# Constants, short loads and bands moved from the set-up into the first FFN, and half of the first weight tiles issued by ScalarE's queue

## The chip, the cores and the metric

The kernel runs on one NeuronCore of a Trainium2 chip, as one program. The metric is the device time in microseconds (us) of one execution; less is better. A core has TensorE (matrix products into PSUM, called PE in the profile, with PEld for its weight loads), VectorE (DVE), ScalarE (ACT), GpSimd (POOL) and SyncE (SP). SP, ACT and POOL also issue transfers, each to a queue of its own (q1, q10 and q0 in the profile), and 16 DMA engines serve all queues.

## The reference

Two transformer-like blocks follow each other on 256 tokens of width 1024, in float32. The first has two layers; beside the tokens `h` it carries 256 context tokens `hc`. Each layer takes nine modulation vectors per stream from `silu(c) @ w_ada`, and is an FFN, a mixer and a second FFN:

```python
# per layer of the first block, m and mc = silu(c) @ w_ada + b_ada for tokens and context
h = post(h, swiglu(pre(h, m, 0, 0), ffn_wi[0], ffn_wo[0]), m, 0, 1, 0.5)
...
h = post(h, o @ w_o, m, 3, 3, 1.0)
h = post(h, swiglu(pre(h, m, 6, 4), ffn_wi[1], ffn_wo[1]), m, 6, 5, 0.5)
```

`pre` is an RMS norm with scale and shift from `m`, `post` a gated residual. The mixer is attention with head gains `qk_g`, rotary tables and, for a group of heads, a relative position bias from `rpb` inside a window; the kernel reads that bias as "bands". The second block is an SSD and mLSTM mixer, a gated linear attention and convolutional FFNs; of it only the small parameters `ab_d_skip`, `ab_dt_bias`, `ab_ig_bias`, `ab_fg_bias` and `ab_a_log` matter here.

## The kernel before

Weights stream through a ring of two slots of 128 x 4096 floats (`RING`, `SLOT`). A float32 product is made of three products of rounded parts: ScalarE copies half a slot (a granule) to `wh` (L453), VectorE subtracts to get `wl` (L458), and TensorE multiplies `uh` x `wh`, `ul` x `wh`, `uh` x `wl` (L467 to L469). Every stage is a block with a program for each engine and a barrier at its end.

**The set-up** (`setup`, L512 on) is the first stage. It needs the token rows, some vectors, and the first six tiles of `w_ada` for layer 0 (1024 rows x 384 columns, 1536 KB each; tiles 0 and 1 in the ring's slots, 2 to 5 in the arena). SP's queue issues the identity (`const[:, 0:P]`, L534), the early vectors (L536), the six ada tiles (L538), and then the two first tiles of the first FFN's weights (L423), each as soon as TensorE is through with the ada tile that held its slot. ScalarE's queue issues four token loads of 512 KB (L618, L619). ScalarE then makes `silu(c)` in `act_c` (L622, L623), issues the rest of the constants (L626, all columns from 128 to 2175) and eight short loads: `head_gain` and `d_skip` twice each with elements of four bytes (L628, L631), three parts of `gate_bias` (L635) and `a_log` (L636). After that it squares the turned tokens (L642). Pool issues the late vectors (L547).

TensorE multiplies `act_c` with one ada tile after the other (`ada_rows`, L666, eight products of 32 output rows each, seen as 16 instructions), turns tokens between the tiles (L568), sums the squares with the constant `ones` after tile 3 (L573; it waits for `const_loaded`), turns the late vectors after tile 4 (L579) and at the end turns the ada rows into columns (L673). VectorE copies the turned tokens to `h` (L603), scales `head_gain` (L610) and puts the modulation vectors into `mod` (L679, L686). Then the barrier comes.

**The first FFN** is `ffn1(0, 0, ...)` (L1248), the next stage. Its norm scales `h` (L826), applies scale and shift on ScalarE (L777), and splits the input into `uh` (L801) and `ul` (L835); before that ScalarE needs the first weight tile (L453), on which VectorE's `wl` and then the first product wait. It has 22 granules of two groups of 128 output columns each; `prod` counts them. Between granules TensorE multiplies one further ada tile (L666). There is one slot for these tiles: ScalarE issues the next (L703) when the products of the last are done, and TensorE needs it after the next granule. Pool runs `load_bands` (L1599) from the stage's start: a flip matrix, a zeroed DRAM buffer (L1607), the `rpb` rows written into it (L1610), each waited for, and then 24 transfers of 64 KB (L1618) from the buffer to `bands`, in runs of 256 bytes. The mixer after this FFN reads them. `ffn1(1, 0, ...)` of layer 1 does the same without ada tiles.

Of the kernel before, what the change touches and what calls it, by code (L numbers as in the profile page):

```python
# [159 lines left out]
def two_blocks(nc, a, out, stop=None):  # L160
    ctx = ExitStack()
    with ctx:
# [4 lines left out]
        def sb(name, shape, dt=F32, at=None):  # L167
            size = 4 * int(np.prod(shape[1:]))
            offset = place[0] if at is None else at
            if at is None:  # L170
                place[0] += (size + 31) // 32 * 32
            return nc.alloc_sbuf_tensor_at(name, shape, dt, offset=offset)

        def signal(name):
            return Signal(ctx.enter_context(nc.semaphore(name)))
# [84 lines left out]
        def col(name, i, n=1):  # L260
# [31 lines left out]
        gelu_done = signal("gelu_done")  # L292
        ada_loaded, ada_multiplied, ada_copied, ada_turned, ada_summed, ada_taken = (signal(n) for n in (
            "ada_tile_loaded", "ada_tile_multiplied", "ada_rows_copied", "ada_columns_made", "ada_columns_summed", "ada_columns_taken"))
        first_loaded, late_loaded, tokens_loaded, const_loaded, gain_loaded, x_squared, x_added, x_summed = (signal(n) for n in (
            "first_vectors_loaded", "late_vectors_loaded", "tokens_loaded", "const_loaded", "gains_loaded", "x_squared", "x_squares_added", "x_summed"))
        low_turned, low_copied, low_weight_loaded, gates_made, gates_biased, gates_softened, decays_summed, decays_made, keys_ended, ends_turned = (
            signal(n) for n in ("low_rank_turned", "low_rank_copied", "low_rank_weight_loaded", "gates_made", "gates_biased", "gates_softened",
                                "decays_summed", "decays_made", "keys_ended", "ended_keys_turned"))
# [172 lines left out]
        def with_lead(eng, n, lead, body, first=0, most=None):  # L472

            turns(eng, n - lead, 4, lambda turn, k: body(turn, k, True), first, most)
            for g in range(n - lead, n):
                body(g // 4, g % 4, False)
# [33 lines left out]
        def setup():  # L512
# [18 lines left out]
            with stage() as block:  # L531
                @block.sync
                def _(sp):
                    sp.dma_start(const[:, 0:P], a["const"][:, 0:P]).then_inc(first_loaded.sem, 16)  # L534
                    for v, t, r, m in early:
                        sp.dma_start(rows[r:r + m, t, :], v).then_inc(first_loaded.sem, 16)  # L536
                    for i in range(ADA_FIRST):
                        sp.dma_start(tiles[i], w_ada[:, :, i * ADA_COLS:(i + 1) * ADA_COLS]).then_inc(ada_ready[i].sem, 16)  # L538
                    for i in range(RING):
                        sp.wait_ge(ada_multiplied.sem, ada_multiplied.at(i + 1))  # L540
                        load(sp, plan[first_key], i, i)
# [7 lines left out]
                @block.tensor  # L549
                def _(pe):  # L550
                    def turned(g):
                        if g >= 3:
                            pe.wait_ge(dve_free.sem, dve_free.at(g - 2))

                    pe.wait_ge(first_loaded.sem, first_loaded.at(16 * (1 + len(early))))
                    for t in range(EARLY):
                        pe.transpose(ps[:, bank_of(t), 0:P], rows[:, t, :], ident).then_inc(prod.sem, 1)
                    pe.wait_ge(act_free.sem, act_free.at(8))
                    for i in range(ADA_FIRST):
                        pe.wait_ge(ada_ready[i].sem, ada_ready[i].at(16))  # L560
                        ada_rows(pe, 0, tiles[i], i, i == 0, i == ADA_FIRST - 1).then_inc(ada_multiplied.sem, 1)
                        for j in TOKENS.get(i, ()):
                            g = EARLY + j
                            if j == 0:
                                pe.wait_ge(tokens_loaded.sem, tokens_loaded.at(16 * 2 * ST))
                            turned(g)
                            for t in range(2 * ST):
                                last = pe.transpose(ps[:, bank_of(g), t * P:(t + 1) * P], tokens[:, t, j * P:(j + 1) * P], ident)  # L568
                            last.then_inc(prod.sem, 1)
                        if i == SUM_AFTER:  # L570
                            pe.wait_ge(const_loaded.sem, const_loaded.at(16))
                            pe.wait_ge(x_added.sem, x_added.at(KD - 1))
                            pe.matmul(ps[:, 7, :], ones, sq_of(0), start=True, stop=True).then_inc(x_summed.sem, 1)  # L573
                        if i == LATE_AFTER:
                            pe.wait_ge(late_loaded.sem, late_loaded.at(16 * len(late)))
                            for t in range(EARLY, len(row_tiles)):
                                g, m = KD + t, row_tiles[t]
                                turned(g)
                                pe.transpose(ps[:, bank_of(g), 0:m], rows[0:m, t, :], ident[0:m, 0:m]).then_inc(prod.sem, 1)  # L579
                    pe.wait_ge(ada_copied.sem, ada_copied.at(1))  # L580
                    ada_columns(pe, 1, mod_rows).then_inc(ada_turned.sem, 1)

                @block.vector
                def _(dve):
# [21 lines left out]
                    add_square(KD - 1)  # L606
                    for t in range(EARLY, len(row_tiles)):
                        take_cols(KD + t, t)
                    dve.wait_ge(gain_loaded.sem, gain_loaded.at(16 * 8))
                    dve.tensor_scalar(head_gain[:, 0::2], head_gain[:, 0::2], HD ** -0.5, None, ALU.mult)  # L610
                    dve.wait_ge(ada_turned.sem, ada_turned.at(1))
                    dve_chain.link(dve, ada_sum(dve, 1, mod_sums))
                    ada_take(dve, mod_sums, 0, ADA_FIRST).then_inc(ada_taken.sem, 1)
# [2 lines left out]
                def _(act):  # L616
                    for t in range(ST):
                        act.dma_start(tokens[:, t, :], a["x"][0, t * P:(t + 1) * P, :]).then_inc(tokens_loaded.sem, 16)  # L618
                        act.dma_start(tokens[:, ST + t, :], a["ctx"][0, t * P:(t + 1) * P, :]).then_inc(tokens_loaded.sem, 16)  # L619
                    act.wait_ge(dve_free.sem, dve_free.at(1))  # L620
                    act.wait_ge(pool_step.sem, pool_step.at(1))
                    act.activation(act_c[:, :, 30], col("c", 0, KD), ACT.Silu).then_inc(act_free.sem, 1)  # L622
                    act.activation(act_c[:, :, 31], col("c_ctx", 0, KD), ACT.Silu).then_inc(act_free.sem, 1)  # L623
                    for _ in range(6):
                        act.nop().then_inc(act_free.sem, 1)
                    act.dma_start(const[:, P:CONST_W], a["const"][:, P:CONST_W]).then_inc(const_loaded.sem, 16)  # L626
                    for half in range(2):
                        act.dma_start(head_gain[half * HD:(half + 1) * HD, :],  # L628
                                      a["qk_g"].rearrange("l i d -> d (l i)"),
                                      allow_slow_non_contiguous=True).then_inc(gain_loaded.sem, 16)  # L630
                        act.dma_start(d_skip[half * HD:(half + 1) * HD, :],  # L631
                                      bass.AP(a["ab_d_skip_2"].tensor, half, [[0, HD], [2, KD]]),
                                      allow_slow_non_contiguous=True).then_inc(gain_loaded.sem, 16)
                    for v, at, n in ((a["ab_dt_bias_2"], 0, 32), (a["ab_ig_bias_2"], 32, 16), (a["ab_fg_bias_2"], 48, 16)):
                        act.dma_start(gate_bias[:, at:at + n], bass.AP(v.tensor, 0, [[0, P], [1, n]])).then_inc(gain_loaded.sem, 16)  # L635
                    act.dma_start(a_log[:, :], bass.AP(a["ab_a_log_2"].tensor, 0, [[0, P], [1, 32]])).then_inc(gain_loaded.sem, 16)  # L636
                    act.preload_act_table_set(LN_EXP)
                    for k in range(KD):
                        act.wait_ge(dve_free.sem, dve_free.at(EARLY + k + 1))
# [605 lines left out]

        spare_beside_bands, spare_of_bands = spare_input("spare_beside_bands", ADA.start), spare_input("spare_of_bands", MID.at)

        def ffn1(l, f, norm, tail, bands_of=None, ada=None, spare=None):  # L1248


            T = norm.T
            key = ("up", l, f)
            down = Down(key, ("down", l, f), mid, T, tail, dve_free, ada, spare)
            pairs = 4 if ada is None else 2
            with stage() as block:
# [40 lines left out]
                def _(dve):  # L1296
# [14 lines left out]
                            down.low_ahead(dve, 1)  # L1311
                    norm.vector(dve, lambda g: low_of(0, g))
                    with_lead(dve, KF, 2, granule)
                    if ada is not None:
                        ada.sums(dve)
                        ada.vector(dve)
                    down.vector(dve)

                @block.gpsimd
                def _(pool):  # L1320
                    if bands_of is not None:
                        load_bands(pool, bands_of)
            norm.done()
            if ada is not None:
                ada.done()
# [1 line left out]
            down.done()  # L1327
            dve_free.passed(KF)
            gate_done.passed(KF)
            if bands_of is not None:  # L1330
                pool_step.passed(1)
                flip_load.passed(16)
                band_load.passed(16 * (2 + B_HEADS * ROWS))
# [261 lines left out]
        assert CC_END <= MID.at and RB.at <= ARENA - (KD + 1) * ADA_COLS and AM.at <= ARENA - B_HEADS * ST * S  # L1595
        bias = Arena(ARENA - B_HEADS * ST * S).take(B_HEADS, ST, S)
        softs = sb("softs", [P, 24])

        def load_bands(pool, l):  # L1599

# [1792 lines left out]
```

## Time and profile before

| | before |
|---|---|
| median of 3 runs | 2850.27 us (2848.3 to 2850.82) |
| profiled execution | 2851.26 us, its span 2849.4 us |
| mean granted TensorE clock | 0.965 |
| TensorE busy | 2681.3 us, 94% of the span |
| VectorE, ScalarE, Pool busy | 1302.6, 1181.2, 42.4 us |
| moved by DMA | 375.50 MB, 132 GB/s over the span |

Times in all views are microseconds from the span's start. A row of an engine gives its start, its length, the line of the kernel, the operation and what it writes and reads; in brackets stands how long the engine had been idle before it and what ended that. The granted clock is given as a share of TensorE's full 2.4 GHz, so 0.50 is its lower level, 1.2 GHz.

### The profile page before, as it was taken

What the parts mean: (1) busy time and instruction counts of PE and PEld (TensorE: products, weight loads), DVE (VectorE), ACT (ScalarE), POOL (GpSimd) and SP (SyncE); (2) the same over time, 40 slices, a digit from 0 to 9 for tenths busy, and PEclk for the clock granted to TensorE, in tenths of its full rate; (3) what the DMA queues carried; (4) which work ended last, traced back from release to release, by engine and by line L of the source; (5) the groups of instructions that cost most, each with busy time, mean ns of one, the idle gap of its engine ahead of it and who ended that gap; (6) DMA issues with size and microseconds to landing.
All of it is one profiled execution on the core that took longest, in us unless ns stands there. A gap on an engine that the chain in (4) does not pass through costs nothing. (4 is left out here: it accounts for less than half of the span.)

```text
span 2849.4 us, 39471 instructions
## 1 busy us (share of the span) xinstructions
PE 2681.3 (94%) x16572; PEld 2288.3 (80%) x16572; DVE 1302.6 (46%) x1659; ACT 1181.2 (41%) x1630; POOL 42.4 (1%) x80
## 2 busy tenths in 40 slices
PE   5999999999899999999999989989977899898999
PEld 2677786877677787788886889989966899897998
DVE  3222235454422234322236564455656576555674
ACT  3222225454422134423226455443355465453664
POOL 2000000000000000100000000000000000000000
PEclk8999999999999999999999999999987999899999
DMA  8666422211466522422222235535500355341453
GB/s 280 209 221 215 159 77 89 60 60 60 148 221 218 203 89 79 108 88 91 109 80 89 60 118 170 184 134 181 179 1 30 119 177 177 136 148 60 148 177 119
DMA packets 277450, 375.50 MB, mean 132 GB/s; under 512 B 11052, under 2 KB 232728, under 8 KB 277184
## 3 DMA queue, kind: packets, MB, share of 16 engines
q1 hardware_dynamic: 228528, 300.50, 31.7%
q10 hardware_dynamic: 46576, 69.26, 7.3%
q0 software_dynamic: 2208, 3.73, 0.8%
q8 instruction: 106, 1.74, 0.3%
q14 instruction: 32, 0.26, 0.0%
HBM read 372.33 MB, written 1.16 MB: 131 GB/s over the span
## 5 line engine op out<-in xcount | busy, mean ns | idle before, releaser
L467 PE MATMUL ps<-uh,wh 128*128 128x256 f32 (+1 forms) x4128 | 1384.3, 335 | 58.6 <-DVE ul L835 38.3
L468 PE MATMUL ps<-ul,wh 128*128 128x256 f32 (+1 forms) x4128 | 1369.1, 332 | 0.0
L469 PE MATMUL ps<-uh,wl 128*128 128x256 f32 (+1 forms) x4128 | 1367.5, 331 | 0.0
L467 PEld LDWEIGHTS ps<-uh,wh 128*128 128x128 f32 x4128 | 794.2, 192 | 172.4 <-issue 54.4
L458 DVE TENSOR_TENSOR wl<-ring,wh 128x2048 fp32r<-128x2048 f32 x210 | 477.4, 2274 | 863.8 <-ACT wh L453 760.6
L469 PEld LDWEIGHTS ps<-uh,wl 128*128 128x128 f32 x4128 | 794.3, 192 | 71.8
L468 PEld LDWEIGHTS ps<-ul,wh 128*128 128x128 f32 x4128 | 795.2, 193 | 68.4 <-issue 0.7
L453 ACT ACTIVATE wh<-ring 128x2048 fp32r<-128x2048 f32 x156 | 298.3, 1914 | 685.9 <-PE ps L469 374.4
L1049 DVE TENSOR_TENSOR wl<-ring,wh 128x2048 fp32r<-128x2048 f32 x66 | 151.3, 2292 | 318.8 <-ACT uh L1067 281.7
L1046 ACT ACTIVATE wh<-ring 128x2048 fp32r<-128x2048 f32 x66 | 126.4, 1915 | 336.0 <-PE ps L469 316.6
L1529 ACT ACTIVATE wh<-ring 128x2048 fp32r<-128x2048 f32 (+2 forms) x38 | 70.0, 1842 | 120.6 <-PE ps L469 120.5
L467 PE MATMUL ps<-wh,uh 128*128 128x256 f32 (+2 forms) x352 | 102.7, 292 | 0.0
L468 PE MATMUL ps<-wl,uh 128*128 128x256 f32 (+2 forms) x352 | 99.9, 284 | 0.0
L469 PE MATMUL ps<-wh,ul 128*128 128x256 f32 (+2 forms) x352 | 99.9, 284 | 0.0
L820 PE MATMUL ps<-arena,const 128*128 128x256 f32 (+1 forms) x144 | 63.9, 604 | 28.9 <-ACT arena L791 28.4
L666 PE MATMUL ps<-arena,act_c 128*32 128x384 f32 x736 | 72.8, 515 | 14.1 <-DMA arena<-in_w_ada_dram 14.1
L820 PEld LDWEIGHTS ps<-arena,const 128*128 128x128 f32 x144 | 34.7, 253 | 57.8 <-ACT arena L791 46.5
L1699 ACT ACTIVATE arena<-ps,softs 128x512 f32<-128x512 f32 (+1 forms) x72 | 43.6, 613 | 77.7 <-DVE softs L1738 62.7
L2226 DVE SCALAR_TENSOR_TENSOR arena<-ps,cols,arena 128x255 f32<-128x255 f32 x176 | 72.5, 474 | 0.0
L467 PEld LDWEIGHTS ps<-wh,uh 128*128 128x128 f32 x352 | 68.3, 194 | 1.9 <-issue 1.5
L468 PEld LDWEIGHTS ps<-wl,uh 128*128 128x128 f32 x352 | 68.3, 194 | 0.9 <-issue 0.7
L469 PEld LDWEIGHTS ps<-wh,ul 128*128 128x128 f32 x352 | 68.4, 194 | 0.0
(335 smaller groups left out, 2086.1 us busy)
## 6 DMA issues: line engine op xcount, KB each, us to landing
ring<-in_ffn_wi_dram SPq DMA_DIRECT2D x88, 1024.0 KB, 7.5
arena<-in_w_ada_dram ACTq DMA_DIRECT2D x42, 1536.0 KB, 6.7
ring<-in_ffn_w_up_dram SPq DMA_DIRECT2D x44, 1024.0 KB, 7.2
ring<-in_ffn_wo_dram SPq DMA_DIRECT2D x20, 2048.0 KB, 7.9
ring<-in_ab_w_in_dram SPq DMA_DIRECT2D x13, 2048.0 KB, 8.0
ring<-in_ffn_w_down_dram SPq DMA_DIRECT2D x10, 2048.0 KB, 7.9
ring<-in_c_w_in_dram SPq DMA_DIRECT2D x6, 2048.0 KB, 7.9
ring<-in_w_in_dram SPq DMA_DIRECT2D x20, 512.0 KB, 5.9
```

The source lines that it names most:

```text
L453: act.activation(shape_of(wh[b]), raw, ACT.Copy).then_inc(high.sem, 1)
L458: dve.tensor_tensor(shape_of(wl[b]), raw, shape_of(wh[b]), ALU.subtract).then_inc(split.sem, 1)
L467: pe.matmul(to, sh, mh, start=start and n == 0, stop=False)
L468: pe.matmul(to, sh, ml, start=False, stop=False)
L469: mm = pe.matmul(to, sl, mh, start=False, stop=stop and last)
L666: last = pe.matmul(ps[q:q + 32, bank, 0:ADA_COLS], act_c[:, kk, ds(30 - 2 * r, 32)], weights[:, kk, :], start=(first and kk < 4), stop=(en ...
L820: last = pe.matmul(self.sum_bank(), ones, self.sq[:, k, :], start=(k == 0), stop=(k == KD - 1))
L1046: return act.activation(wh[side(self.key, g)][:, :], self.weights(g), ACT.Copy)
L1049: return dve.tensor_tensor(wl[side(self.key, g)][:, :], self.weights(g), wh[side(self.key, g)][:, :], ALU.subtract)
L1529: act.activation(shaped(wh[side(key, g)]), raw, ACT.Copy).then_inc(high.sem, 1)
L1699: ins = act.activation(probs[:, s % 2, e, c], ps[:, 3 + e, c], ACT.Exp, bias=self.small(0, s, 4)[:, i:i + 1], accum_out=self.small(1, s, 4 ...
L2226: ins = dve.scalar_tensor_tensor(out=conv_buf[:, q, part, to], in0=ps[:, 2 * q + part, of], scalar=channel("ffn_conv_w", tap, part, g), in ...
```

## The change

The first 256 columns of the constants (identity and `ones`) are loaded by SP at the start, so that TensorE's wait for `const_loaded` goes. The rest of the constants and the eight short loads leave the set-up and become `load_late`, issued by Pool in the first FFN of layer 0 after the bands. `load_bands` itself now first waits for the fourth granule of products (`BANDS_AT`), in both layers. VectorE's scaling of `head_gain` moves with the loads to the end of that FFN's granules. Of the six ada tiles of the set-up, SP issues 0, 2, 4 and ScalarE's queue 1, 3, 5: tile 1 after the tokens, tiles 3 and 5 after `silu(c)`.

```diff
# setup
-                    sp.dma_start(const[:, 0:P], a["const"][:, 0:P]).then_inc(first_loaded.sem, 16)
+                    sp.dma_start(const[:, 0:2 * P], a["const"][:, 0:2 * P]).then_inc(first_loaded.sem, 16)
...
-                    for i in range(ADA_FIRST):
+                    for i in range(0, ADA_FIRST, 2):
                         sp.dma_start(tiles[i], w_ada[:, :, i * ADA_COLS:(i + 1) * ADA_COLS]).then_inc(ada_ready[i].sem, 16)
...
                         if i == SUM_AFTER:
-                            pe.wait_ge(const_loaded.sem, const_loaded.at(16))
                             pe.wait_ge(x_added.sem, x_added.at(KD - 1))
...
-                    dve.wait_ge(gain_loaded.sem, gain_loaded.at(16 * 8))
-                    dve.tensor_scalar(head_gain[:, 0::2], head_gain[:, 0::2], HD ** -0.5, None, ALU.mult)
...
+                    def odd_tile(i):
+                        act.dma_start(tiles[i], w_ada[:, :, i * ADA_COLS:(i + 1) * ADA_COLS]).then_inc(ada_ready[i].sem, 16)
+
+                    odd_tile(1)
                     act.wait_ge(dve_free.sem, dve_free.at(1))
...
-                    act.dma_start(const[:, P:CONST_W], a["const"][:, P:CONST_W]).then_inc(const_loaded.sem, 16)
...
+                    for i in range(3, ADA_FIRST, 2):
+                        odd_tile(i)
# ffn1
                     with_lead(dve, KF, 2, granule)
+                    if late:
+                        dve.wait_ge(rest_loaded.sem, rest_loaded.at(16 * LATE_LOADS))
+                        dve.tensor_scalar(head_gain[:, 0::2], head_gain[:, 0::2], HD ** -0.5, None, ALU.mult)
...
                     if bands_of is not None:
+                        pool.wait_ge(prod.sem, prod.at(BANDS_AT))
                         load_bands(pool, bands_of)
+                    if late:
+                        load_late(pool)
+                        pool.wait_ge(rest_loaded.sem, rest_loaded.at(16 * LATE_LOADS))
# new
+        def load_late(pool):
+            pool.dma_start(const[:, 2 * P:CONST_W], a["const"][:, 2 * P:CONST_W]).then_inc(rest_loaded.sem, 16)
+            for half in range(2):
+                pool.dma_start(head_gain[half * HD:(half + 1) * HD, :],
+                               a["qk_g"].rearrange("l i d -> d (l i)"), allow_slow_non_contiguous=True).then_inc(rest_loaded.sem, 16)
+                pool.dma_start(d_skip[half * HD:(half + 1) * HD, :],
+                               bass.AP(a["ab_d_skip_2"].tensor, half, [[0, HD], [2, KD]]),
+                               allow_slow_non_contiguous=True).then_inc(rest_loaded.sem, 16)
+            for v, at, n in ((a["ab_dt_bias_2"], 0, 32), (a["ab_ig_bias_2"], 32, 16), (a["ab_fg_bias_2"], 48, 16)):
+                pool.dma_start(gate_bias[:, at:at + n], bass.AP(v.tensor, 0, [[0, P], [1, n]])).then_inc(rest_loaded.sem, 16)
+            pool.dma_start(a_log[:, :], bass.AP(a["ab_a_log_2"].tensor, 0, [[0, P], [1, 32]])).then_inc(rest_loaded.sem, 16)
```

## Rows read from the trace of the kernel before

**Rows 1.** The page: busy us, share of the span, instructions.
```profile
PE 2681.3 (94%) x16572; PEld 2288.3 (80%) x16572; DVE 1302.6 (46%) x1659; ACT 1181.2 (41%) x1630; POOL 42.4 (1%) x80
```

**Rows 2.** Busy time by stretch; at the end granted clock, DMA share, GB/s.
```profile
20.00:30.00 10.00, 4.35 (x28) 1.98 (x28) 4.38 (x7) 4.84 (x7) 0.00 (x0) 0.71 0.62 183
34.00:42.00 8.00, 5.71 (x44) 2.19 (x42) 3.93 (x9) 2.58 (x4) 0.00 (x0) 0.98 1.06 375
62.00:72.00 10.00, 10.00 (x54) 7.29 (x53) 5.57 (x6) 5.36 (x9) 10.00 (x18) 1.00 0.76 94
...
88.00:90.00 2.00, 2.00 (x16) 0.43 (x12) 0.00 (x0) 0.00 (x0) 0.00 (x0) 0.50 0.00 0
...
100.00:150.00 50.00, 50.00 (x257) 37.18 (x256) 11.56 (x8) 12.28 (x10) 0.00 (x0) 1.00 0.61 198
```

**Rows 3.** Timeline, 45 to 57 us: start, length, engine, line, operation, idle before.
```profile
45.02 2.79 PE L666 MATMUL ps<-arena,act_c 128*32 128x384 f32 x16 [2.95 <-DMA arena<-in_w_ada_dram]
...
50.17 0.17 DVE L881 TENSOR_SCALAR pre_scale<-mod 128x16 f32<-128x16 f32 x1 [0.39 <-PEq L531]
...
51.02 1.91 ACT L453 ACTIVATE wh<-ring 128x2048 fp32r<-128x2048 f32 x1 [2.66 <-DMA ring<-in_ffn_wi_dram]
...
56.51 0.79 PE L467 MATMUL ps<-uh,wh 128*128 128x512 f32 x1 [7.55 <-DVE ul L835]
```

**Rows 4.** Timeline of TensorE: groups of ada products (L666).
```profile
39.43 1.50 PE L666 MATMUL ps<-arena,act_c 128*32 128x384 f32 x16 [0.81 <-DMA arena<-in_w_ada_dram]
...
70.03 1.50 PE L666 MATMUL ps<-arena,act_c 128*32 128x384 f32 x16
...
87.84 2.79 PE L666 MATMUL ps<-arena,act_c 128*32 128x384 f32 x16 [5.17 <-DMA arena<-in_w_ada_dram]
...
102.55 1.50 PE L666 MATMUL ps<-arena,act_c 128*32 128x384 f32 x16
...
165.37 1.50 PE L666 MATMUL ps<-arena,act_c 128*32 128x384 f32 x16
...
177.95 1.50 PE L666 MATMUL ps<-arena,act_c 128*32 128x384 f32 x16
```

**Rows 5.** Line 703, the FFN's 21 ada loads, 0 to 450 us: issue to landing.
```profile
DMA to landing us min/median/max: 6.4/6.6/16.1
```

**Rows 6.** Timeline of Pool: the 24 band transfers.
```profile
61.39 14.61 POOL L1618 DMA_DIRECT2D arena<-rpb_padded  x24 [3.78 <-DMA rpb_padded<-in_rpb_dram]
```

**Rows 7.** Queues from 20 to 30 us: packets, MB, share of 16 engines.
```profile
q1 hardware_dynamic: 1211, 1.82, 56.2%
q10 hardware_dynamic: 1213, 0.01, 6.2%
```

**Rows 8.** Timeline of the queues' issues in the set-up (SPq, ACTq).
```profile
6.03 25.12 SPq L538 DMA_DIRECT2D arena<-in_w_ada_dram  x4
...
14.29 3.43 ACTq L635 DMA_DIRECT2D gate_bias<-in_ab_dt_bias_dram  x1
```

**Rows 9.** Queues from 82 to 86 us.
```profile
q10 hardware_dynamic: 614, 0.94, 63.3%
q1 hardware_dynamic: 580, 0.59, 42.2%
```

**Rows 10.** Queues from 76 to 81 us.
```profile
q0 software_dynamic: 249, 0.52, 49.7%
q10 hardware_dynamic: 260, 0.40, 32.0%
```

**Rows 11.** Timeline of VectorE in the set-up.
```profile
42.23 0.16 DVE L610 TENSOR_SCALAR head_gain<-head_gain 128x2 f32<-128x2 f32 x1
```

**Rows 12.** TensorE's waits, 700 to 740 us: us, times, longest.
```profile
PE ps L820 <- ACT arena L791: 4.9, 1, 4.9
```

**Rows 13.** TensorE's waits, 1120 to 1160 us, the start of layer 1.
```profile
PE ps L820 <- ACT arena L791: 4.5, 1, 4.5
```

More of the change, by code:

```diff
@@ L294, in two_blocks @@
             "ada_tile_loaded", "ada_tile_multiplied", "ada_rows_copied", "ada_columns_made", "ada_columns_summed", "ada_columns_taken"))
-        first_loaded, late_loaded, tokens_loaded, const_loaded, gain_loaded, x_squared, x_added, x_summed = (signal(n) for n in (
-            "first_vectors_loaded", "late_vectors_loaded", "tokens_loaded", "const_loaded", "gains_loaded", "x_squared", "x_squares_added", "x_summed"))
+        first_loaded, late_loaded, tokens_loaded, rest_loaded, x_squared, x_added, x_summed = (signal(n) for n in (
+            "first_vectors_loaded", "late_vectors_loaded", "tokens_loaded", "rest_loaded", "x_squared", "x_squares_added", "x_summed"))
         low_turned, low_copied, low_weight_loaded, gates_made, gates_biased, gates_softened, decays_summed, decays_made, keys_ended, ends_turned = (
@@ L625, in _ @@
                         act.nop().then_inc(act_free.sem, 1)
-                    act.dma_start(const[:, P:CONST_W], a["const"][:, P:CONST_W]).then_inc(const_loaded.sem, 16)
[L627 to L636, printed above, removed]
+                    for i in range(3, ADA_FIRST, 2):
+                        odd_tile(i)
                     act.preload_act_table_set(LN_EXP)
@@ L1246, in two_blocks @@
         spare_beside_bands, spare_of_bands = spare_input("spare_beside_bands", ADA.start), spare_input("spare_of_bands", MID.at)
+        BANDS_AT = 4
         def ffn1(l, f, norm, tail, bands_of=None, ada=None, spare=None):
             T = norm.T
+            late = (l, f) == (0, 0)
             key = ("up", l, f)
@@ L1329, in ffn1 @@
             gate_done.passed(KF)
+            if late:
+                rest_loaded.passed(16 * LATE_LOADS)
             if bands_of is not None:
@@ L1597, in two_blocks @@
         softs = sb("softs", [P, 24])
+        LATE_LOADS = 9
+        def load_late(pool):
[9 more added lines that the diff above has]
+            pool.dma_start(a_log[:, :], bass.AP(a["ab_a_log_2"].tensor, 0, [[0, P], [1, 32]])).then_inc(rest_loaded.sem, 16)
         def load_bands(pool, l):
```

## Prediction

> **What bounds the kernel now.** I read the page first: TensorE is busy 94% of the span [rows 1], so a transfer can only move the time where TensorE waits for it. The next view is the busy time by stretch. From 100 to 150 us TensorE is busy in all 50 us with the DMA engines at a share of 0.61, so there they have some 39% to spare; from 34 to 42 us it is the other way round: a DMA share of 1.06 at 375 GB/s and TensorE with holes [rows 2]. So the set-up is bound by transfers and the first FFN by TensorE. Two places are left where the change can act.
>
> The first is the **end of the set-up**. The timeline shows the last ada tile reaching TensorE at 45.02, the next stage's first operation at 50.17, and ScalarE starting on the first FFN weight tile at 51.02, which it waited for; the first FFN product starts at 56.51 [rows 3]. The chain is: DMA engines full until 51.0, then 5.5 us of splitting and norm.
>
> The second is **one ada tile in the first FFN**. Its groups of row products start at 70.03, 87.84 and 102.55, and later at 165.37 and 177.95 [rows 4]. The undisturbed period is 177.95 - 165.37 = 12.58 us; the two disturbed ones take 32.52 instead of 25.16, a loss of 7.4 us. It consists of 5.17 us of waiting for the ada tile, 2.79 - 1.50 = 1.3 us because the group then ran with a granted clock of 0.50 [rows 2], the 1.2 GHz level, after TensorE had stood idle, and 0.9 us for the slow products after it. The tile took 16.1 us to land where 6.6 is usual [rows 5], while the Pool queue was issuing the 24 band transfers from 61.39 on, 14.61 us long [rows 6].
>
> **Part 1: the removed traffic of the set-up.** The constants without the first 256 of their 2176 columns are 1920 x 128 x 4 bytes, 0.98 MB; at 375 GB/s [rows 2] that is 2.6 us. The short loads carry almost no bytes but much time. From 20 to 30 us the DMA moved 183 GB/s at a share of 0.62 [rows 2], and the queue view says why: SP's queue (q1) sent 1211 packets and ScalarE's queue (q10) 1213, the latter with 0.01 MB in all [rows 7]. The two queues took turns, a weight packet for a four-byte packet. That costs (375 - 183) x 10 / 375 = 5.1 us. Both traffics leave a stretch that was full to its end, so the first FFN tile lands 2.6 + 5.1 = 7.7, with the thinner edges of that stretch 7.8 us earlier, at 43.2. The 64 KB of `ones` that SP now loads ahead are 0.2 us of a part that ends before TensorE's first tile; I count nothing.
>
> **Part 2: every second tile on ScalarE's queue.** SP spends 25.12 us issuing four tiles [rows 8], so it is stuck behind a full queue, not short of time: the engines' share is already 1.06. I count 0 for bandwidth. The Trainium skill (DMA: Bandwidth & Descriptors, Issuing engines are not separate DMA queues) says the same against this half of the change: all queues run on the same 16 engines, and a second issuer saves issue time only; by that rule it is worth 0, and if SP's blocked 25 us were lost transfer time it would be worth microseconds more.
> What it does change is the order. ScalarE's queue holds four token loads and tiles 1, 3, 5; SP's holds tiles 0, 2, 4 and then the FFN tile. Two queues with work send equal packet counts: 614 against 580 from 82 to 86 us [rows 9]. So tile 5 no longer lands ahead of the FFN tile by a whole tile: with 4.7 MB on either queue after the tokens, tiles 4 and 5 land close together, near 38 us. TensorE gets a denser chain (six groups of 1.50 to 2.79 us [rows 4], three rounds of turned tokens between them) and should start the last one at about 38.5 to 39. From that group to the next stage's first operation took 5.15 us [rows 3], so the stage starts near 43.9 and ScalarE is ready 0.4 us later or, with the last groups at the higher clock, 1.3 us sooner. Against 43.2 for the FFN tile I take 43.9 for both: 51.02 - 43.9 = **7.1 us gained**, bounds 2.3 (below, rival D) and 7.8. ScalarE can be held by a full queue (one short load took 3.43 us to issue [rows 8]), but tile 5 is issued before it has a square to make; its cover is that the first turned tokens come after tile 0. If that cover goes, the sum of squares is late, ahead of group 4.
>
> **Part 3: the bands leave the stage's start.** The 7.4 us above go away: nothing else is late there, because the FFN tiles have two slots. **7.4 us gained**, bounds 6.5 and 7.4.
>
> **Part 4: the bands come back four granules in.** Pool now waits for the fourth granule of products; behind that wait are only the loads, and nobody waits for Pool before the end of the stage, hundreds of us later. In the old coordinates it comes after 115; the band transfers start 61.39 - 50.17 = 11.2 us later [rows 3, 6] and run 14.6 us, longer than one period, so one ada tile is always beside them. A tile is needed 12.58 - 1.50 = 11.1 us after its issue and lands after 6.6 [rows 4, 5]: slack 4.5. It is 1.57 MB, 4.2 us at full rate, so 2.4 of the 6.6 are start-up. Low bound: contending, the bands held 49.7% of the engines' time [rows 10], which leaves 188 GB/s: 8.4 + 2.4 = 10.8 us, no stall. High bound: left to themselves they kept the share at 0.76 [rows 2], which leaves 90 GB/s: 1.08 MB in 12 us, the rest in 1.3, landing after 15.7, a stall of 4.6 plus 2.1 of slow clock, 6.7. The tail of an FFN tile makes a third queue for part of it, and then the ada tile got 0.40 MB in 5 us [rows 10]. I take the middle, **3.5 lost**.
>
> **Part 5: nine late loads behind the bands.** The constants take 2.6 us of the engines, the four-byte packets again take turns. Beside them alone a tile moves at 183 GB/s [rows 2]: 8.6 + 2.4 = 11.0 us, just in time; with constants or an FFN tile in the same period it is late. Bounds 0 and one more late tile at the old price, 7.4; **1.5 lost**, near the low end because the one measured rate just fits. The Trainium skill (DMA: Bandwidth & Descriptors, Rules for kernel authors) says that a strided last dimension becomes one descriptor per element; by it moving these loads makes none cheaper and the upper bound is the likelier, which is rival C.
>
> **Part 6: what counts as nothing.** VectorE's scaling of `head_gain` is 0.16 us [rows 11] and moves between the last granule and the ada sums; behind it wait the sums and two banks that TensorE fills last, microseconds of cover. TensorE's removed wait for the constants ended long before. In layer 1 the bands move too: TensorE's wait for the norm's squares was 4.5 us at that stage's start, beside the bands' first transfers, and 4.9 in the stage at 700 us that loads no bands [rows 12, 13]. Zero.
>
> **The sum.** -7.1 - 7.4 + 3.5 + 1.5 = **-9.5 us**. The profiled execution took 2851.26 (span 2849.4 and 1.9 around it), 1.0 over the median 2850.27: it becomes 2841.8, and the median 2840.8.
>
> **The rivals.**
> **A, the forecast**, chance 0.52: bands and late loads together cost 2 to 8.5 us, the set-up gives 6.5 to 7.8: 2837.1 to 2844.9.
> **B, the moved transfers are hidden altogether**, 0.22: -7.1 - 7.4 = -14.5, 2835.8. For it: 39% spare engine time and 188 GB/s beside the bands. Against it: the tile that took 16.1 us.
> **C, the stall moves and doubles**, 0.11: one tile late by the bands (6.7), one by the late loads (6.1): -14.5 + 12.8, 2848.6. For it: 11.0 us against 11.1 allowed.
> **D, the order of the queues eats the set-up's gain**, 0.10: tile 5, behind the tokens and issued by an engine that other work can hold, lands with the last byte at 43.2 instead of ahead of the FFN tile; then 43.2 + 5.15 + 0.4 = 48.7 replaces 51.02, 2.3 gained: -2.3 - 7.4 + 5.0, 2845.6. For it: no row shows ScalarE's queue with weights beside SP's from the start. Against it: equal turns. The Trainium skill (same page, Queues, rings and completion order) has each engine go round its queues packet by packet, which also speaks against D; the trace agrees with 614 to 580.
> **E, slower**, 0.05: the ada tile has one buffer, and each late tile delays the next issue. If the four-byte packets stretch so that three tiles in a row land late at the old 7.4, it is -14.5 + 22.2 = +7.7, 2858.0. It decides from stalls of 14.5 us on, two full late tiles.
>
> **How the numbers follow.** The point is A's, 2840.8. The range leaves out C and E and keeps the others: 2835.0 to 2847.5. A measurement of this kernel can tell about 0.2%, 5.7 us, from no change. Faster by more: nearly all of A (0.49), B, and 0.04 of D: 0.75. Within: the rest of A and D, C: 0.21. Slower by more: 0.04.
>
> **What would show it.** Part 1: no stretch between 18 and 32 us under 300 GB/s. Part 2: the first FFN product near 49.4 instead of 56.51, and the FFN tile and the stage's start within 1 us of each other; if ScalarE starts on that tile only around 48.7, D holds. Part 3: the second ada group of the FFN 12.6 us after the first. Parts 4 and 5: one or two ada groups between 115 and 170 us behind a wait on their tile, one of them by 1 to 4 us; none is B, three is E. From there on every stage is shifted alike. The prediction is wrong if the shift changes after 200 us, for nothing there is touched but layer 1's bands.

## The result, and the profile after

| | before | changed |
|---|---|---|
| median of 20 runs each | 2848.71 us | 2853.18 us |
| lowest to highest | 2843.9 to 2852.0 | 2850.29 to 2857.01 |
| profiled execution, its span | 2851.26, 2849.4 | 2857.01, 2855.2 |

The changed kernel is 0.2% slower: ratio 1.002, 95% interval 1.0014 to 1.0026; the medians are 4.5 us apart. The forecast was 2840.8, 9.5 us faster, with a range up to 2847.5. (The three runs shown ahead of the prediction are the first of the 20 of before.) The executions of one kernel differ among themselves by 8.1 us before and by 6.7 after, and both profiled executions are among the longest of their kernel, so that a difference of two spans says less than the medians do; one execution of the first experiment took 6725 us and is not counted.

The timeline of the changed kernel at the end of the set-up answers to [rows 3], with the last rows of the set-up's ada groups (L658 is the old L666):

```profile
37.09 2.79 PE L658 MATMUL ps<-arena,act_c 128*32 128x384 f32 x16 [3.02 <-DMA arena<-in_w_ada_dram]
...
41.06 1.50 PE L658 MATMUL ps<-arena,act_c 128*32 128x384 f32 x16
...
44.94 0.17 DVE L873 TENSOR_SCALAR pre_scale<-mod 128x16 f32<-128x16 f32 x1 [0.40 <-PEq L531]
45.37 1.91 ACT L453 ACTIVATE wh<-ring 128x2048 fp32r<-128x2048 f32 x1 [2.25 <-PEq L531]
...
50.86 0.79 PE L467 MATMUL ps<-uh,wh 128*128 128x512 f32 x1 [7.14 <-DVE ul L827]
```

The first product comes at 50.86 instead of 56.51: 5.65 us gained. ScalarE's wait for the FFN tile is gone; what ended its idle time is the stage's barrier (PEq L531). The set-up is now bound by TensorE's chain from the late tile 4 on, not by the FFN tile. Four other traces with this same set-up (below) have the product at 51.58 to 51.78, and two at 50.81 and 50.88, so that it gives 4.7 to 5.7 us.

The ada groups of the first FFN, where [rows 4] stood for before:

```profile
63.30 1.50 PE L658 MATMUL ps<-arena,act_c 128*32 128x384 f32 x16
76.85 1.50 PE L658 MATMUL ps<-arena,act_c 128*32 128x384 f32 x16 [0.90 <-DMA arena<-in_w_ada_dram]
89.42 1.50 PE L658 MATMUL ps<-arena,act_c 128*32 128x384 f32 x16
...
114.55 1.50 PE L658 MATMUL ps<-arena,act_c 128*32 128x384 f32 x16
132.17 2.76 PE L658 MATMUL ps<-arena,act_c 128*32 128x384 f32 x16 [4.97 <-DMA arena<-in_w_ada_dram]
...
153.65 2.79 PE L658 MATMUL ps<-arena,act_c 128*32 128x384 f32 x16 [7.25 <-DMA arena<-in_w_ada_dram]
...
168.96 1.50 PE L658 MATMUL ps<-arena,act_c 128*32 128x384 f32 x16
```

Set against the same groups of before, the lead grows and is then lost:

| ada group | before | changed | difference |
|---|---|---|---|
| first | 70.03 | 63.30 | -6.7 |
| second | 87.84 | 76.85 | -11.0 |
| third | 102.55 | 89.42 | -13.1 |
| sixth | 140.27 | 132.17 | -8.1 |
| seventh | 152.80 | 153.65 | +0.9 |
| eighth | 165.37 | 168.96 | +3.6 |

After the eighth both kernels keep the period of 12.58. So 13.1 us were won by the third group, and three long periods after the fifth (17.62, 21.48 and 15.31, together 54.4 instead of 37.7) took 16.7 back. The Pool queue's timeline puts two things beside them:

```profile
111.30 14.61 POOL L1636 DMA_DIRECT2D arena<-rpb_padded  x24 [4.50 <-DMA rpb_padded<-in_rpb_dram]
131.81 0.56 POOL L1606 DMA_DIRECT2D const<-in_const_dram  x1 [5.90 <-DMA arena<-rpb_padded]
132.36 0.62 POOL L1608 DMA_DIRECT2D head_gain<-in_qk_g_dram  x1
132.97 0.69 POOL L1610 DMA_DIRECT2D d_skip<-in_ab_d_skip_dram  x1
```

ScalarE issues one ada tile into the bands and the next into the late loads:

```profile
116.24 0.38 ACTq L695 DMA_DIRECT2D arena<-in_w_ada_dram  x1
135.10 0.39 ACTq L695 DMA_DIRECT2D arena<-in_w_ada_dram  x1
```

The second is the surprise. The busy time by stretch, and Pool's queue in the same stretch (packets, MB, share of 16 engines), for 136 to 142 us:

```profile
136.00:142.00 6.00, 6.00 (x28) 4.94 (x27) 2.89 (x2) 2.02 (x2) 1.12 (x3) 1.00 0.85 10
```
```profile
q0 software_dynamic: 121, 0.06, 85.5%
```

A DMA share of 0.85 and 10 GB/s: for 6 us the engines are occupied and move almost nothing, not even the ada tile issued at 135.10. Only Pool's queue has packets there.

The span grew by 5.8 us, 2.2 more than the FFN. That part is spread over later stages that the change leaves alone, in steps of 1 to 2 us up and down. The page's group of the norms' sums shows one place that may hold some of it: 144 products took 66.3 us here and 63.9 in the profile of before (line 812, old 820), 2.4 us more.

```profile
L812 PE MATMUL ps<-arena,const 128*128 128x256 f32 (+1 forms) x144 | 66.3, 625 | 28.9 <-ACT arena L783 28.4
```

It is no effect of the change that I can show: the kernel with only the bands' wait (below) has its FFN within 0.2 us of before and a span 4.2 us shorter. In layer 1, where the bands were moved too, TensorE's waits from 1100 to 1300 us are 4.7 and 4.5 us in both kernels.

### The profile page after: what moved, and what is told of

It is laid out like the page before. It is cut to its first block and busy times, and to the rows that moved or that the text cites. A ratio compares the mean times of both kernels' runs of the same rounds, so it can differ in the third digit from the quotient of the medians.

```text
span 2855.2 us, 39470 instructions
## 1 busy us (share of the span) xinstructions
PE 2681.7 (94%) x16572; PEld 2289.2 (80%) x16572; DVE 1302.7 (46%) x1659; ACT 1181.8 (41%) x1630; POOL 47.7 (2%) x89
## 5 line engine op out<-in xcount | busy, mean ns | idle before, releaser
L812 PE MATMUL ps<-arena,const 128*128 128x256 f32 (+1 forms) x144 | 66.3, 625 | 28.9 <-ACT arena L783 28.4
L658 PE MATMUL ps<-arena,act_c 128*32 128x384 f32 x736 | 72.7, 515 | 16.8 <-DMA arena<-in_w_ada_dram 16.8
```

Of the source, the lines that this page charges most:

```text
L658: last = pe.matmul(ps[q:q + 32, bank, 0:ADA_COLS], act_c[:, kk, ds(30 - 2 * r, 32)], weights[:, kk, :], start=(first and kk < 4), stop=(en ...
L812: last = pe.matmul(self.sum_bank(), ones, self.sq[:, k, :], start=(k == 0), stop=(k == KD - 1))
```

## The experiments

Times of the runs are ratios to the kernel before on the same chip; for the changed kernel that ratio is 1.0020. 0.1% is 2.8 us.

### The element loads left out

```diff
-LATE_LOADS = 9
+LATE_LOADS = 5      # no head_gain, no d_skip; both filled with ones
```

> The changed kernel without the four loads of head_gain and d_skip (1536 elements of four bytes); both tiles are filled with ones instead, so the head gains and the skip weights are left out of the computation. Theory 'elements': issued by Pool, 32 such elements travel as one packet that holds a DMA engine for 3.6 to 4.8 us, and that made the ada tile after the bands late (wait 7.25 us, then one slow group and one long period). Then that wait goes, the wait of 5 us beside the bands stays, and the kernel is 8 to 10 us faster than the changed one, some 4 to 5 us faster than before. Rival 'bytes or knock-on': the 0.98 MB of constants, or the first late tile, made the second one late; then at most 2 us are gained.

Ratio 0.9996 (0.9986 to 1.0006), about 7 us faster than the changed kernel, a little less than expected. TensorE's groups:

```profile
134.43 2.79 PE L660 MATMUL ps<-arena,act_c 128*32 128x384 f32 x16 [5.60 <-DMA arena<-in_w_ada_dram]
148.83 1.50 PE L660 MATMUL ps<-arena,act_c 128*32 128x384 f32 x16
161.40 1.50 PE L660 MATMUL ps<-arena,act_c 128*32 128x384 f32 x16
```

The wait beside the bands stays at 5.6 us and the next tile is in time, although the 0.98 MB of constants still follow the bands. So neither the bytes nor the first late tile made the second one late. The periods that end at the first two of these groups are 18.25 (the group before is at 116.18) and 14.40, 7.5 us over two usual ones: the price of the bands. The other 16.7 - 7.5 = 9.2 us are the element loads'.

### Which elements

```diff
-LATE_LOADS = 9
+LATE_LOADS = 7      # first kernel: no d_skip; second kernel: no head_gain
```

> The changed kernel without the two d_skip loads alone (1024 elements of four bytes, in which 64 partitions read the same 8 addresses each); d_skip is filled with ones, so the skip weights are left out of the computation. Theory 'repeated addresses': the packets of 3.6 to 4.8 us are d_skip's, 128 bytes each, while head_gain's packets of 64 bytes took 25 ns. Then no packet above 1.5 us is left and the second late ada tile is in time: 7 to 10 us faster than the changed kernel. Rival 'all four-byte elements': a wait of 2 us or more stays there.

> The changed kernel without the two head_gain loads alone (512 elements of four bytes at distinct addresses); head_gain is filled with ones, so the head gains are left out of the computation. Theory 'repeated addresses': nothing changes, the packets of 3.6 us and the wait of some 7 us stay, within 1.5 us of the changed kernel. Rival 'all four-byte elements': the wait shortens by about a third, 2 to 3 us.

Without `d_skip`: 0.9986 (0.9975 to 0.9996), 9 to 10 us faster than the changed kernel. Without `head_gain`: 1.0033 (1.0019 to 1.0047), no gain; the interval overlaps that of the changed kernel. Their groups, first without `d_skip`, then without `head_gain`:

```profile
133.16 2.79 PE L659 MATMUL ps<-arena,act_c 128*32 128x384 f32 x16 [4.93 <-DMA arena<-in_w_ada_dram]
147.89 1.50 PE L659 MATMUL ps<-arena,act_c 128*32 128x384 f32 x16
```
```profile
132.68 2.79 PE L659 MATMUL ps<-arena,act_c 128*32 128x384 f32 x16 [4.96 <-DMA arena<-in_w_ada_dram]
151.95 2.79 PE L659 MATMUL ps<-arena,act_c 128*32 128x384 f32 x16 [5.37 <-DMA arena<-in_w_ada_dram]
```

It is `d_skip`. In its source 64 partitions read the same eight addresses; `head_gain` has equally small elements at 256 different ones. One expectation missed in part: without `head_gain` the second wait is 5.37 and not 7.25 us in this profile, and the three long periods take 13.5 us over the usual instead of 16.7, so `head_gain` may hold 3 us as long as `d_skip` is there too; the times do not show them. With `d_skip` alone left out the excess is 7.2, about that of the bands; the longest packet left on Pool's queue took 1.7 us, where at most 1.5 were expected.

### The kernel before with the short loads on Pool's queue

```diff
                     for v, t, r, m in late:
                         pool.dma_start(rows[r:r + m, t, :], v).then_inc(late_loaded.sem, 16)
+                    for half in range(2):
+                        pool.dma_start(head_gain[half * HD:(half + 1) * HD, :],
...
-                    for half in range(2):
-                        act.dma_start(head_gain[half * HD:(half + 1) * HD, :],
...
```

The cut lines are the rest of the eight short loads, the same on both sides.

> The kernel before with its eight short loads of the set-up issued by Pool after the late vectors instead of by ScalarE. Theory 'elements': 1536 four-byte elements on Pool's queue hold the engines for about 10 us with nothing moving beside them, where ScalarE's queue let a weight packet through after each element and cost 5.1: the first FFN product comes 3 to 6 us later than 56.5 and the kernel is as much slower. Rival 'the queue makes no difference': within 1.5 us of before.

1.0018 (1.0009 to 1.0028), and the first product at 59.57 instead of 56.51: the loads alone, moved from one queue to another within the set-up, cost 3.1 us in the trace and about 5 in the times, whose interval (2.6 to 8.0 us) holds the 3.1. Pool also issues them some 3 us earlier (the first at 8.72 instead of 11.54), so that the place is not quite the old one, and the rival "the queue makes no difference" is out. The queues from 14 to 22 us, here and in the kernel before:

```profile
q0 software_dynamic: 77, 0.01, 78.3%
q1 hardware_dynamic: 237, 0.36, 12.6%
q10 hardware_dynamic: 13, 0.11, 3.2%
```
```profile
q1 hardware_dynamic: 1054, 1.59, 58.4%
q10 hardware_dynamic: 790, 1.05, 36.5%
```

The first three lines are this run's, the last two those of the kernel before. 77 packets with 0.01 MB hold 78.3% of 16 engines for 8 us, and the weight queue gets 0.36 MB through where it had 1.59.

### The late loads first, by Pool and by SP

```diff
-                    if bands_of is not None:
-                        pool.wait_ge(prod.sem, prod.at(BANDS_AT))
-                        load_bands(pool, bands_of)
                     if late:
                         load_late(pool)
                         pool.wait_ge(rest_loaded.sem, rest_loaded.at(16 * LATE_LOADS))
+                    if bands_of is not None:
+                        pool.wait_ge(prod.sem, prod.at(BANDS_AT))
+                        load_bands(pool, bands_of)
```

In the second kernel SP calls `load_late` ahead of its FFN tiles and Pool only waits for it.

> The changed kernel with the nine late loads issued by Pool at the first FFN's start, ahead of the bands, which still wait for the fourth granule. Theory 'place': the elements hold the engines from about 47 to 62 us, when the next ada tile is not needed before 63 and the next FFN tile not before 66, so at most one short wait shows there; the wait beside the bands (7 us in all) stays. Some 9 us faster than the changed kernel, 4 to 7 us faster than before. Rival 'any place costs': the loads that the held engines delay at the start cost as much as later, so within 2 us of the changed kernel.

> As the run with the late loads first, but SP issues them, ahead of its FFN tiles. Theory 'packets': on SP's queue every element is a packet of its own, so that the trace shows other queues' packets between them and no packet of some 3.6 to 4.8 us; time as with Pool's queue within 2 us, since both places are covered. Rival 'the loads are slow on any queue': packets of microseconds here too.

0.9978 (0.9969 to 0.9987) and 0.9979 (0.9970 to 0.9988): both about 6 us faster than before, within the 4 to 7 expected, and 12 faster than the changed kernel, where 9 were expected. By the eighth ada group the trace of Pool's version is 8.6 us ahead of the changed kernel's (160.35 against 168.96); the rest lies in later stages and is not explained. In the first granule, where the next ada tile has been issued 18 us before it is needed, the same loads are followed by no wait above 0.7 us until the bands come. So the rival "any place costs" is out. In SP's kernel the queues from 51 to 56 us are

```profile
q10 hardware_dynamic: 640, 0.98, 61.7%
q1 hardware_dynamic: 638, 0.00, 6.4%
```

640 weight packets against 638 element packets: on this queue every element is a packet of its own and lets one of the other queue through. Read one by one, the packets of the two queues are:

```
loads of d_skip and head_gain     packets of        median time of one
Pool's queue, changed kernel      32 x 128 B        3619 ns (longest 4764)
                                  32 x 64 B           25 ns
SP's queue, this run              1536 x 4 B           7 to 9 ns (longest 14)
```

On Pool's queue 32 elements go as one packet, and one packet of `d_skip` holds its engine for 3.6 us, 113 ns an element. The `d_skip` load on SP's queue reads the same repeated addresses and has no long packet, so repeated addresses alone do not make one.

### Only the bands' wait

```diff
                     if bands_of is not None:
+                        pool.wait_ge(prod.sem, prod.at(4))
                         load_bands(pool, bands_of)
```

> The kernel before with one edit: Pool waits for the fourth granule before it loads the bands. Theory 'the stall only moves': the 7.4 us lost at the second ada group go and 7 us come back at the sixth: within 2 us of before. Rival 'in the changed kernel the bands met the late loads': without these the bands are nearly hidden there, 4 to 7 us faster than before.

1.0004 (0.9994 to 1.0014), no change. The second group now waits 0.66 us, the sixth 5.46:

```profile
138.46 2.79 PE L666 MATMUL ps<-arena,act_c 128*32 128x384 f32 x16 [5.46 <-DMA arena<-in_w_ada_dram]
152.97 1.50 PE L666 MATMUL ps<-arena,act_c 128*32 128x384 f32 x16
```

The two periods there are 18.11 and 14.51, 7.5 over the usual. The stall moves in full, with no late load near it. (The group before these is at 120.36.)

### The bands after the last ada tile

```diff
-                        pool.wait_ge(prod.sem, prod.at(BANDS_AT))
+                        pool.wait_ge(prod.sem, prod.at(KF if late else BANDS_AT))
```

on top of the late loads first, by Pool.

> Late loads first by Pool, and in layer 0 the bands wait for the last (22nd) granule, after the last ada tile. Theory 'the one buffer': bands cost time only where an ada tile must land within one granule, so here they cost nothing, and the whole of 5.7 (first product) + 1.1 (shorter slow clock after it) + 7.4 (old stall) less up to 2 shows: 11 to 14 us faster than before, 16 faster than the changed kernel. Rival 'the bands always delay a weight tile': a wait of several us shows in the second half of the FFN, and at most 8 us are gained.

0.9960 (0.9946 to 0.9974), 11 us faster, the low end of what was expected, median 2836.71 against 2849.83; the eighth ada group is at 152.39, 13.0 before that of [rows 4]. TensorE's waits from 40 to 350 us:

```profile
PE ps L658 <- DMA arena<-in_w_ada_dram: 1.0, 1, 1.0
```

where the changed kernel has

```profile
PE ps L658 <- DMA arena<-in_w_ada_dram: 13.1, 3, 7.2
```

The bands run from 334 us on beside the FFN's second half, at a DMA share of 0.85 with TensorE busy in 16 of 16 us (334 to 350), and TensorE waits for no tile up to 460 us.

### All six tiles by SP

```diff
-                    for i in range(0, ADA_FIRST, 2):
+                    for i in range(ADA_FIRST):
...
-                    odd_tile(1)
...
-                    for i in range(3, ADA_FIRST, 2):
-                        odd_tile(i)
```

Once in the changed kernel, once on top of the bands after the last ada tile.

> The changed kernel with all six ada tiles of the set-up on SP's queue again. Theory 'order': bandwidth is the same, but in one queue the last ada tile lands one FFN tile (5.7 us) ahead of the FFN tile's end at 42.9, so that the stage starts at about 42.3 and the first FFN product comes near 48.5 instead of 50.86: 2 to 2.5 us faster than the changed kernel. Rival 'two queues move more': the FFN tile lands later, and the first product comes at 51 or later.

> As the run before it, and all six ada tiles of the set-up on SP's queue. Theory 'order': the first product comes near 48.2 instead of 50.9, and with no late tile behind it the 2.5 us stay: 13 to 17 us faster than before. Rival 'the gain of the order is taken back in the FFN': same as the run with the odd tiles on ScalarE's queue, within 1 us, though the first product is earlier.

The first product comes at 48.23 and 48.43, 2.4 to 2.6 us earlier, as expected. The first is

```profile
48.23 0.80 PE L467 MATMUL ps<-uh,wh 128*128 128x512 f32 x1 [7.54 <-DVE ul L824]
```

In the changed kernel this did not reach the time, and the expected 2 to 2.5 us failed: 1.0018 (1.0008 to 1.0027) against 1.0020. The lead is 1.6 us at the first ada group (61.67 against 63.30) and 0.5 at the eighth, with 14.0 us of waits for ada tiles instead of 13.1. The issuing queue makes no difference to the bandwidth: from 24 to 32 us SP's queue alone moves 373 GB/s here, as much as the two queues together in the changed kernel.

```profile
q1 hardware_dynamic: 1966, 2.97, 105.4%
```

On top of the kernel with the bands at the end the median is 2834.39 against 2836.71 and the ratio 0.9950 (0.9936 to 0.9964) against 0.9960; the intervals overlap, so that these 2.3 us are likely and not shown. This is the fastest version: 14 to 15 us faster than before, 19 to 20 faster than the change.

## Why the prediction was wrong

**Parts 1 and 2, the set-up, were right in the mechanism and a little too large.** 7.1 us were forecast; 5.65 show at the first product, and 6.7 at the first ada group, because fewer products there ran at the lower clock than before. Part of the 6.7 is luck: five of the seven traces with this set-up have that group at 64.7 to 65.1 and not at 63.3, 5.0 to 5.3 us gained. From 18 to 34 us no stretch of 2 us is under 372 GB/s, as part 1 said. The stage began at 44.94 where I had 43.9: TensorE waited 3.02 us for tile 4, ran that group at the lower clock and only then reached tile 5, at 41.06 instead of 38.5 to 39. The 0 for bandwidth held (373 GB/s by one queue and by two). But the split over two queues cost 2.5 us by its order: with all six tiles by SP the last group starts at 36.75. The prediction saw this order and priced it at 0.7 us, 43.9 instead of 43.2.

**Part 3 was right in the main**: past the 6.7 us of the set-up the lead grew by 4.3 at the second group and by 2.1 more at the third, 6.4 in all of the old stall of 7.4, just under its lower bound of 6.5; 0.9 remained as a short wait, with no band near it. That tile was issued at 65.00, and from 65 to 69 us the queues were

```profile
q1 hardware_dynamic: 1122, 1.13, 89.0%
q10 hardware_dynamic: 1, 0.00, 0.1%
```

FFN tiles on SP's queue held the engines for the first 4 us, and the ada tile started only then. The tile of the old stall was issued at 71.73 in the kernel before, and there the queues from 72 to 76 us were

```profile
q1 hardware_dynamic: 988, 1.00, 84.4%
q0 software_dynamic: 69, 0.14, 12.4%
q10 hardware_dynamic: 7, 0.01, 1.0%
```

So the old stall began with the same late start behind FFN tiles; alone it costs 0.9 us, and with the bands 7.4.

**Part 4 took the wrong end.** The bands' return was priced at 3.5, the middle of 0 and 6.7; 7.5 was measured twice (18.11 and 14.51; 18.25 and 14.40), the old price of [rows 4] again. The low bound let an ada tile have 188 GB/s beside the bands. From 122 to 130 us the queues were

```profile
q0 software_dynamic: 449, 0.92, 55.4%
q10 hardware_dynamic: 674, 1.03, 48.4%
```

1.03 MB in 8 us, 129 GB/s; and from 116 to 120 us, after its issue at 116.24, the tile had sent two packets while the bands and an FFN tile held the engines. So it landed after some 16 us and not 10.8. The row that decided was in my hands: the one tile that had met the bands was late by 7.4. I called that start a special case of three queues; there was an FFN tile at the new place too.

**Part 5 failed, and alone turned the sign.** It priced the late loads at 1.5 with a bound of 7.4; they cost 9.2 in the trace. The step that failed is "beside them alone a tile moves at 183 GB/s": that row was measured with the loads on ScalarE's queue, where each element alternates with a weight packet [rows 7], and I carried it to Pool's queue, where 32 go at once and no tile moves at all. The change of queue was in the diff; no row showed `d_skip` on Pool's queue, and a price from another queue was no bound for it. The Trainium skill (DMA: Bandwidth & Descriptors, Queues, rings and completion order) says that an engine drains a whole packet of many descriptors before it turns to another queue; I had used the rule against rival D only. The runs agree with it: 121 packets held 85.5% of the engines for 6 us, single ones for 3.6 us, and the tile beside them sent nothing.

**The sum.** -6.7 - 6.4 + 7.5 + 9.2 = +3.6 us at the eighth group, against -9.5. The medians say +4.5. The prediction also called itself wrong if the shift changed after 200 us: in the profiles it goes from 3.6 to 5.8, but with only the bands' wait it goes from 0.2 to -4.2, so that this sign tells nothing of the change. Rival C had the right places (one tile late by the bands, one by the late loads) at 12.8 instead of 16.7; it takes E's threshold, stalls above 14.5, to come out slower, and that was passed. The mechanism of C and the sign of E together had 0.16.

**Part 6 held.** `head_gain` is scaled at 350.66 in 0.17 us and no one waits for it; layer 1's waits are the same in both kernels.

What stays open: the 113 ns for an element of `d_skip` were tied to the load, by leaving it out, not to its repeated addresses. These are the likely difference to `head_gain` on Pool's queue, where a packet also has 32 elements instead of 16; a `d_skip` read from distinct addresses was not run. Why FFN tiles hold back an ada tile for 4 us in some granules, though the two queues share evenly elsewhere, and why later stages differ by some microseconds between kernels with the same code there, was not tried.

## What to carry to other kernels

A transfer moved to another queue is another transfer: its price beside other traffic has to be taken from a row of that queue. Where one buffer must be refilled within one step, look for that deadline first and put everything else on the DMA engines where no such refill is under way (here after the last ada tile, and in the first granule); a transfer moved from beside one such deadline to beside another cost the same again here (7.4 and 7.5 us). Small loads belong where work whose data has already landed covers them; their bytes say little of their price.

## What the runs showed of the hardware

Two loads of together 1024 four-byte elements (`d_skip`), issued by Pool, were 32 packets of about 3.6 us each, some 7 us on each of the 16 engines; from 136 to 142 us all queues together moved 10 GB/s, and a weight tile issued just before did not start. With `head_gain`'s 512 elements and issued by SP they were 1536 packets of 7 to 9 ns that alternated one to one with the weights (640 and 638 in 5 us). SP's and ScalarE's queues, with equal packets, shared the engines evenly and moved 373 GB/s together from 24 to 32 us of the changed kernel, but not in every stretch (1122 to 1 from 65 to 69 us):

```profile
q10 hardware_dynamic: 988, 1.49, 53.0%
q1 hardware_dynamic: 985, 1.49, 52.9%
```
